# One sum of squares later and undivided, three settling products fewer and two more, and the activations 64 bytes lower in memory

## The reference, cut to what matters

```
h = x
h = h + gmlp_mixer(rmsnorm(h), ...);            h = h + conv_ffn(rmsnorm(h), ...)
h = h + chunk_attention(rmsnorm(h), k, v, ...); h = h + conv_ffn(rmsnorm(h), ...)
x = rmsnorm(h)
h = h + sb_rwkv_mixer(rmsnorm_2(x), ...);       h = h + conv_glu(rmsnorm_2(h), ...)
e = rmsnorm_2(p[0] @ ple_w_proj[0]); h = h + sigmoid(rmsnorm_2(h) @ ple_w_gate[0]) * e
h = h + mla_mixer(rmsnorm_2(h), ...);           h = h + conv_glu(rmsnorm_2(h), ...)
e = rmsnorm_2(p[1] @ ple_w_proj[1]); h = h + sigmoid(rmsnorm_2(h) @ ple_w_gate[1]) * e
return rmsnorm_2(h)
```

## Time and profile before

| | |
|---|---|
| median of 3 runs | 1300.93 us (1300.87 to 1302.28) |
| the profiled execution, its own time | 1301.2 us |
| its span, first to last instruction | 1299.3 us |
| PE busy | 1271.3 us, 98% of the span |
| DVE busy | 918.1 us, 71% |
| ACT busy | 757.4 us, 58% |
| mean busy share of the DMA engines | 46% |

### The profile page before, as it was taken

How to read it: one execution, slowest core, us unless ns; L and a number is a source line. 1 busy time by engine, 2 the same in 40 slices (tenths; PEclk the granted TensorE clock), 3 DMA queues, 4 the chain that set the end, 5 groups by cost and what they waited for, 6 DMA issues and landing times.

```text
span 1299.3 us, 29241 instructions
## 1 busy us (share of the span) xinstructions
PE 1271.3 (98%) x12180; PEld 1238.1 (95%) x12180; DVE 918.1 (71%) x1314; ACT 757.4 (58%) x980; POOL 40.0 (3%) x34
## 2 busy tenths in 40 slices
PE   9999999999999999999999999999999999999997
PEld 8999999998899999998988999999998889999997
DVE  4789886488479886488656477665587779666557
ACT  6667665367667665368544266554465876554444
POOL 1010000010010000000000010000010001000000
PEclk9999999999999999999999999999999999999999
DMA  8455555555345555545302036555534335555520
GB/s 339 167 223 195 194 194 194 194 195 197 129 162 195 194 194 197 194 163 185 131 34 85 18 138 227 194 194 205 194 132 152 130 127 201 210 194 194 194 98 33
DMA packets 31980, 220.61 MB, mean 170 GB/s; under 512 B 3712, under 2 KB 3840, under 8 KB 6160
## 3 DMA queue, kind: packets, MB, share of 16 engines
q1 hardware_dynamic: 30672, 213.36, 45.2%
q0 software_dynamic: 784, 4.85, 1.0%
q10 hardware_dynamic: 432, 1.05, 0.2%
HBM read 218.20 MB, written 1.05 MB: 169 GB/s over the span
## 4 chain that ended last, share of the span: by engine, by line
PE 83%; DVE 10%; ACT 5%; issue 1%; DMA 1%; POOL 0%; SPq 0%; DVEq 0%; ACTq 0%; POOLq 0%
PE ps L1901 21%; PE ps L1903 20%; PE ps L1902 20%; PE ps L1912 16%; DVE w_lo L1119 3%; ACT w_hi L507 2%; PE ps L1907 2%; PE ps L1909 2%; PE ps L1908 2%; DVE xt L1171 1%; PE ps L2143 1%; DVE xA L1182 1%; DMA raw<-stream 1%; ACT L525 0%; DVE xB L1182 0%
## 5 line engine op out<-in xcount | busy, mean ns | idle before, releaser
L1119 DVE TENSOR_TENSOR w_lo<-raw,w_hi 128x2048 fp32r<-128x2048 f32 x197 | 449.9, 2288 | 141.0 <-ACT w_hi L507 140.8
L507 ACT ACTIVATE w_hi<-raw 128x2048 fp32r<-128x2048 f32 x197 | 376.6, 1915 | 160.2 <-PE ps L1903 155.9
L1901 PE MATMUL ps<-xB,w_hi 128*128 128x256 f32 x1120 | 311.9, 278 | 0.0
L1902 PE MATMUL ps<-xB,w_hi 128*128 128x256 f32 x1120 | 309.8, 277 | 0.0
L1903 PE MATMUL ps<-xB,w_lo 128*128 128x256 f32 x1120 | 309.8, 277 | 0.0
L1901 PE MATMUL ps<-xA,w_hi 128*128 128x256 f32 x744 | 210.0, 282 | 2.0 <-DVE gl L1526 1.6
L1901 PEld LDWEIGHTS ps<-xB,w_hi 128*128 128x128 f32 x1120 | 210.6, 188 | 1.3 <-issue 0.9
L1902 PEld LDWEIGHTS ps<-xB,w_hi 128*128 128x128 f32 x1120 | 210.3, 188 | 0.1
L1903 PEld LDWEIGHTS ps<-xB,w_lo 128*128 128x128 f32 x1120 | 210.3, 188 | 0.0
L1903 PE MATMUL ps<-xA,w_lo 128*128 128x256 f32 x744 | 206.4, 277 | 0.0
L1902 PE MATMUL ps<-xA,w_hi 128*128 128x256 f32 x744 | 206.4, 277 | 0.0
(11 more groups left out here) (316 smaller groups left out, 1856.5 us busy)
## 6 DMA issues: line engine op xcount, KB each, us to landing
raw<-stream SPq DMA_DIRECT2D x199, 1024.0 KB, 4.8
raw<-stream SPq DMA_DIRECT2D x4, 512.0 KB, 7.8
at_bias<-rel POOLq DMA_DIRECT2D x1, 2048.0 KB, 8.1
hT<-x_t SPq DMA_DIRECT2D x4, 256.0 KB, 6.8
lora_w<-lora POOLq DMA_DIRECT2D x1, 1024.0 KB, 5.5
out_t<-xt SPq DMA_DIRECT2D x4, 256.0 KB, 2.6
hcon<-hyc POOLq DMA_DIRECT2D x1, 576.0 KB, 3.9
wsT<-wst ACTq DMA_DIRECT2D x1, 512.0 KB, 4.4
```

Of the source, the lines that this page charges most:

```text
L507: nc.scalar.activation(w_hi[c.slot][:], raw[c.slot][:], ACT.Copy).then_inc(hi_made, 1)
L1119: nc.vector.tensor_tensor(w_lo[c.slot][:], raw[c.slot][:], w_hi[c.slot][:].bitcast(F32), ALU.subtract).then_inc(lo_made, 1)
L1901: nc.tensor.matmul(out, wh, xh, start=start, stop=False, skip_group_check=True)
L1902: nc.tensor.matmul(out, wh, xl, start=False, stop=False, skip_group_check=True)
```

## The change

- `x_offset` has 96 bytes a partition instead of 160. All activations lie 64 bytes lower; they start 128 bytes under a multiple of a weight tile's 512 bytes.
- N_ML leaves `SUM_APART`: both sums of the norm ahead of the MLA stand before k = 5 of its early pair, none before k = 4.
- `sum_first(N_FF2)` loses its product of 64 columns.
- In `ffn`, pair 2 keeps the settling product ahead of its first chunk; those ahead of the second chunk (ffn(2) and ffn(3)) go.
- In `ple`, both products for e stand before k = 3 of g = 1, and a settling product is put ahead of g = 2, in both calls.

```diff
-SUM_APART = (N_FF0, N_AT, N_FF1, N_ML, N_FF3)
+SUM_APART = (N_FF0, N_AT, N_FF1, N_FF3)
...
-        sb("x_offset", [P, 40])
+        sb("x_offset", [P, 24])
...
                 pe.wait_ge(sq_folded, FOLD_AT[n] + 1)
-                if n == N_FF2:
-                    plain(half(4, 0)[:, 0:64], ones, ones[:, 0:64])
                 plain(half(4, 0), ones, xt[:, 6, :], True, False)
...
-                    if settled[0]:
+                    if settled:
                         settle(2 * par)
                     wide_chunk(cu, 2 * par, x, ready)
                     if ready is None:
                         pe.wait_ge(gate_conv, q + (base - 1))
-                    if settled[1]:
-                        settle(2 * par + 1)
                     wide_chunk(cg, 2 * par + 1, x)
...
-                pair(2, 0, Chunk(c0 + 4), Chunk(c0 + 5), None, (True, f >= 2))
+                pair(2, 0, Chunk(c0 + 4), Chunk(c0 + 5), None, True)
...
-                def e_first():
+                def e_sums():
                     pe.wait_ge(e_folded, i + 1)
                     plain(half(5, 1), ones, pl_sq[:, 4, :], True, False)
-
-                def e_second():
                     plain(half(5, 1), ones, pl_sq[:, 5, :], False, True).then_inc(e_ss, 1)
...
-                    early = {3: e_first, 4: e_second} if g == 1 else {}
+                    early = {3: e_sums} if g == 1 else {}
+                    if g == 2:
+                        settle(GATE_BANK[g])
```

More of the change, by code:

```diff
@@ L2037, in ffn, with pair @@
                 up_used = up_conv if both else prod_made
-                def pair(q, par, cu, cg, ready=None, settled=(False, False)):
+                def pair(q, par, cu, cg, ready=None, settled=False):
                     if ready is None:
                         pe.wait_ge(up_used, q + (base - 1))
-                    if settled[0]:
+                    if settled:
                         settle(2 * par)
```

## The result

The changed kernel takes 1337.18 us (median of 4 runs, 1336.57 to 1338.96) against 1301.16 us for the kernel before (1300.87 to 1302.28): a ratio of 1.028, 95% interval 1.0265 to 1.0295, so 36 us more where I had forecast 5 less. The profiled execution took 1338.96 us, with a span of 1337.1.

The account below looks back on a forecast made before the run. PE's matmul stream was taken as the bound. From 1301.2 us: -3.04 (N_ML), 0 (settling), -0.10 (64 columns), -0.02 (products for e) and -2.0 (address) gave 1296 us, range 1290 to 1302.

Parts of the forecast that it names:

- What bounds the kernel: Whole kernel: PE's matmul stream sets the time, at two lasting paces, 113.3 and 117.8 ns; the slow one costs 6.2 us.
- The addresses: Activations moved by 64 bytes: a third of the 6.2 us of slow pace gained, 2.0 us.
- another pace: All PE streams: the new place lets matmuls go at 109 ns, some 38 us less, 1260 us; chance 0.04.
- The rival that ends slower: Pair 2 of an ffn: a settling product no longer brings the fast pace, 6.1 us a loop, 1303.8 to 1322; chance 0.1.
- The rule against any effect of the address: PE's operand reads: ports never wait and are independent, so the address term is 0, giving 1297.7 us; chance 0.2.
- The 109.2 ns: PE's streams: the skill's 262 cycles for 256 columns at 2.4 GHz, a pace no stream of the trace reaches.
- Both sums ahead of k = 5: Norm ahead of the MLA: k = 4 runs in PE's wait, saving 3.04 us if the clock stays up.
- The 1.7 us for the fallen clock: Ahead of the MLA: the half-clock part of the 3.04 us gain, beside 1.36 us of moved work.
- The settling products: ffn(2), ffn(3) and the gated parts: two go, two come, 0.22 us each, net 0.
- The 64 columns: Product ahead of the sum at N_FF2, removed: 0.10 us saved, bound 0.
- the products for e: Both in one piece in the two ple calls: one interruption instead of two, 0.02 us saved for both calls.

Follow-up runs that it names:

- f1: The kernel before with N_ML out of SUM_APART, nothing else: 1301.34 us against 1303.40, ratio 0.9980.
- g3: The changed kernel with 160 unused bytes and the second settling products of ffn(2) and ffn(3) put back: 1300.45 us against 1303.05, ratio 0.9979.
- g4: The kernel before with N_ML out of SUM_APART and no product of 64 columns at N_FF2: 1300.11 us against 1303.05, ratio 0.9981.
- f2: Label not tied in the text; by order probably the kernel before without the second settling products of ffn(2) and ffn(3): 1302.26 us, ratio 1.0000.
- f4: Label not tied in the text; by elimination probably the kernel before with 416 unused bytes (320 under a weight tile): 1304.21 us, ratio 0.9999.
- f3: Label not tied in the text; by order probably the kernel before with none of the eight settling products: 1308.36 us, ratio 1.0054.
- e2: The changed kernel with 160 unused bytes again, all program edits kept: 1302.61 us against 1302.64, ratio 0.9995.
- e3: Label not tied in the text; by order probably the kernel before with 96 unused bytes and 64 ahead of the weight buffers: 1336.64 us, ratio 1.0262.
- e4: Label not tied in the text; by order probably the kernel before with 224 unused bytes (level with a weight tile): 1347.46 us, ratio 1.0345.
- g1: Label not tied in the text; by order probably the kernel before with 64 unused bytes (160 under a weight tile): 1347.68 us, ratio 1.0348.
- g2: Label not tied in the text; by order probably the kernel before without the unused tensor (224 under a weight tile): 1324.06 us, ratio 1.0167.

## Why the prediction was wrong

**What bounds the kernel** was right: it is the pace of PE's stream, and the two paces and their persistence over a stretch showed up in every profiled kernel with 64 or 320 bytes. The "little over a fifth" that PE was busy before the clock fell is a quarter (0.64 of 2.5 us).

**The step that failed is "The addresses".** I wrote that nothing in the trace shows another offset, "so the price has to be bounded", and then bounded it by the paces that the trace showed at 64 bytes: -6.2 us if all became fast, +6.1 us for a loop that turns slow. A new distance has paces of its own, and the rival "another pace" was worked out only downwards (its 38 us would be 48 by the 9,553 steps). The 5,580 matmuls of the loops alone, 5.4 ns slower each, are 30 us; all streams are 43 us, as 9,550 steps at 4.5 ns, of which the waits give some back. Measured alone, the term is +36.3 us (1338.95 - 1302.64) where I had -2.0. It lies outside both bounds, and above all four loops together (+24 us). A bound worked out from the one value that a trace shows says nothing of the others. The profile did show that nearly all could be lost: all but 162 us of the streams went at the better of two paces, so a move had far more room upwards than down. An estimate from those rows was there to be had: the other 928 us of the streams at 117.8 ns would be 37 us more. The rival that ends slower had a chance of 0.1 and another mechanism.

**The rule against any effect of the address** (the Trainium skill, "SBUF — State Buffer", section "SBUF: two separate sides", and "TensorE: Matmul & The Clock Gate", "Step-by-step: what each phase is for") gave 0 for this term. The runs give 36.3 us, so the measurement decides against it here. The 109.2 ns that I worked out from the 262 cycles of the Trainium skill ("TensorE: Matmul & The Clock Gate", "Back-to-back issue gap") was reached by no long stream at any of the distances; 113.3 was the least.

**Both sums ahead of k = 5**: the mechanism was right at 64 bytes and is seen in the traces of f1, g3 and g4, where PE idles 0.65 to 0.67 us as forecast. The size is 2.1 us alone (0.8 to 4.6 by the interval), which does not rule out the 3.04. The 1.7 us for the fallen clock are those of one execution. Of the profiled executions with the sums apart and 64 or 320 bytes, the clock fell there in before, f2 and f4 and not in f3; in f1, e2, g3 and g4, with both sums ahead of k = 5, in none. At the other distances it fell there in none of the nine with the sums apart either. So that this part of the saving is there only when the fall would have been is likely, and not shown by itself.

**The settling products**: the cost of 0.22 us is a reading of the trace that no run measured alone. The sum "two go, two come: 0" left out what I had named as their cover. In e2 a loop entered through a single product went at 117.8 ns, 6.3 us, which is the slower rival's mechanism; its price per loop, 6.1 us, was right. "All eight lead there now" was read from one execution. In the changed kernel itself they don't lead to the fast pace, since at 128 bytes no stream has it.

**The 64 columns and the products for e** were too small to be told apart by any run here.

## What to carry to other kernels

In this kernel's streams (float32r, the type of the split parts, `fp32r` in the views; 128x128 by 256 columns, new weights for each matmul) the distance in memory between the moving and the stationary operand, by 256 bytes, is a parameter of the pace. In a kernel of this kind, sweep it with a tensor nobody uses, and look at the count of matmuls in a window, not at the busy time. Any other edit that changes the size of a tensor in between moves it, so check it again after each. Where a trace shows one value of such a parameter, its price at another has no bound from that trace; change it alone and measure.

## What the runs showed of the hardware

- The same matmul of 128x128 by 256 columns, at full clock, was started every 113.3, 116.6, 117.4, 117.8, 118.3, 118.7 or 120.0 ns, by the distance of its operands and by what interrupted the stream last. With 64 bytes there are two lasting paces, 113.3 and 117.8 ns; with 96 and 128 there is more than one as well.
- The pace is the same at 64 and 320 bytes under, and at 192 under and 64 above, and it did not change when both operands moved together by 64 bytes (118.7 and 118.8 ns). It changes sides when the operands change roles.
- PE's granted clock fell to half (1.2 of 2.4 GHz) for 3.4 us at some of its waits: ahead of the fall at 982.5 us in before it had been busy for 0.64 of 2.5 us, ahead of the one at 789.6 us in f1 for 1.42 of 2.6. The same wait brought a fall in one kernel's execution and none in another's; at half clock, 3.4 us hold what takes 1.7 at full clock. In the profiled executions it fell between zero times (e3, e4, g1, g4) and three (after, e2, f1, f2, f3, f4, g2) ahead of the last stage.
- Why the pace depends on the distance stays open; the trace shows only the starts. Distances between the steps of 32 bytes, and how often a settling product loses the fast pace, stay open as well.
